# Two mixers read the raw stream; their norm's root is multiplied in behind the projections

## The chip, the cores and the metric

The kernel runs on 1 core of a Trainium2 chip. The metric is the time of one execution on the device, in microseconds (us); where several executions are timed, their median. Six things work side by side in the core, each through its own instruction list in order: TensorE (PE in the profile, with its weight loads as PEld), VectorE (DVE), ScalarE (ACT), GpSimd (POOL) and the queue on SyncE (SP) that issues the transfers. They meet only through semaphores: an instruction can be told to wait until another engine has counted one up.

## What is computed

Two transformer blocks run one after the other on one sequence of 256 tokens with 1024 features. Block 1 has a mixer and a feed-forward part. Block 2 has two layers; layer 0 mixes with a short convolution beside a forgetting attention, layer 1 with a conformer convolution module, and each is followed by a gated feed-forward part. Cut to what the change touches:

```python
def rms_norm_2(x, g):
    xf = x.astype(jnp.float32)
    y = xf * lax.rsqrt(jnp.mean(xf * xf, axis=-1, keepdims=True) + RMS_EPS)
    return (y * g.astype(jnp.float32)).astype(x.dtype)

def shortconv_fox_mixer(h, w_in, b_f, conv_w, w_out):
    proj = h @ w_in
    gate_b = proj[..., OFF_GB:OFF_GC]
    gate_c = proj[..., OFF_GC:OFF_XA]
    xa = proj[..., OFF_XA:OFF_Q]
    y_a = gate_b * causal_depthwise_conv(gate_c * xa, conv_w)
    ...
    log_f = jax.nn.log_sigmoid((proj[..., OFF_F:] + b_f).astype(jnp.float32))
    y_b = forgetting_attention(q, k, v, log_f).reshape(bsz, seq, D_FOX)
    return jnp.concatenate([y_a, y_b.astype(h.dtype)], axis=-1) @ w_out

def conformer_conv_module(h, w_pw1, b_pw1, w_dw, b_dw, ln_g, ln_b, w_pw2, b_pw2):
    a, g = jnp.split(h @ w_pw1 + b_pw1, 2, axis=-1)
    u = a * jax.nn.sigmoid(g)
    ...

def second_block(x, ...):
    h = x
    for layer in range(DEPTH_2):
        u = rms_norm_2(h, norm_mix_pre[layer])
        m = shortconv_fox_mixer(u, ...) if layer % 2 == 0 else conformer_conv_module(u, ...)
        h = h + rms_norm_2(m, norm_mix_post[layer])
        f = swiglu_ffn(rms_norm_2(h, norm_ffn_pre[layer]), w_ffn_in[layer], w_ffn_out[layer])
        h = h + rms_norm_2(f, norm_ffn_post[layer])
    return h
```

The norm divides every token by one number, its root. A matrix product is linear, so that factor may be applied to the product's result as well as to its input.

## The kernel before, in words

**Numbers in two halves.** Every large product is made of float32 numbers split into a high and a low part; three matrix multiplications (high·high, high·low, low·high) stand for one. The stream's halves lie in `H[0]` and `H[1]` (shown as H_h, H_l), 8 chunks of 128 features by 256 tokens. Weights arrive by DMA in units of 1 MB in the `raw` buffers; ACT copies a unit to `whi` (`split_hi`, L343), DVE subtracts to get `wlo` (`split_lo`, L350). There are two buffers of each, so the split of a unit waits until the unit two before it has been multiplied. `next_hi` and `next_lo` split the unit that follows the one named.

**Order of the work.** Each engine's list is written out by hand: `pe_program`, `act_program`, `dve_program` call one function per stage in the same order. The stages here are named after their weights: `down` (end of block 1), then layer 0's mixer `mix0` (`win2` units 6 to 11, the forget gate `wf2`, `win2` 0, then a run of eight attention jobs between which the remaining `win2` units are filled in), `wout2`, the feed-forward `ffn0` (`f0`, `g0`), layer 1's mixer `mix1` (`pw1`, the convolution by Fourier transform, a layer norm, `pw2`), and `ffn1` (`f1`, `g1`).

**From stage to stage.** A stage that ends in `wide_pe` (L1527) leaves its product in four PSUM banks, a token half `t` by a feature half `cb` each. DVE multiplies each by a row of gains (`mg_dve`, L1614, into `Mt`) and adds it to the stream `X` (`x_dve_add`, L1622, L1625); `X` has tokens on the partitions. PE turns `X` around (`turn_k`, L1652, a transpose of 128 by 128), ACT writes H_h with the norm's gain (`spread_act`, L1687), DVE writes H_l (`spread_dve`, L1692), and the next projection begins. `turnx_pe` does 12 of 16 transposes; the last four are a hook inside the first projection, which runs chunk by chunk as H arrives. While PE would wait, `spin_pe` (L432) makes it multiply for nothing.

**Two ways to norm.** Before `mix0` and `mix1` the norm is taken first: ACT squares `X` (L1542), makes the roots (`root_act`, L1551, L1554), and ACT and DVE write `X` times its root into `Mt` (`xs_act` L1564, `xs_dve` L1568); the transposes read `Mt`. Before `ffn0` and `ffn1` the transposes read `X` itself; ACT squares and takes the roots later, behind the next unit's split, PE makes a tile of them with one column per token (`rn_pe`, L1703, after the second projection unit), ACT copies it to `rn` (`rn_act`, L1711), and DVE multiplies `rn` in as it empties PSUM (L1837).

**Emptying PSUM in the mixers.** In `mix0` ACT empties most projections (`fox_act`, L1876 to L1889: gbt, gct, fq, fk), DVE only the values `fv` (L1910) and the product of the second gate (L1901). In `mix1` ACT takes the sigmoid of one half of a unit (L2210) and DVE multiplies the other half by it (L2243), both straight from PSUM.

Of the kernel before, what the change touches and what calls it, by code (L numbers as in the profile page):

```python
# [151 lines left out]
def build(nc, ins, out):  # L152
# [79 lines left out]
    place[0] = block2  # L232
    gbt, gct = sb("gbt", [128, 4, 256]), sb("gct", [128, 4, 256])
# [976 lines left out]
    def score_pe(pe, jobs, j, free):  # L1210
# [365 lines left out]
    def out_act(act, name, post, gen, scale):  # L1576
# [222 lines left out]
    def down_dve(dve):  # L1799
# [5 lines left out]
        out_dve(dve, "down", False, "mix0", True, lambda cb: mod_set(21 + 2 * cb), between)  # L1805
# [8 lines left out]
    def ffn_act(act, n, gen, name, rn_free=()):  # L1814
        for c in range(NF):
            next_hi(act, (n, c))
            if c == 0:
                for t in range(2):
                    xsq_act(act, name, gen, t, 0)
                    xsq_act(act, name, gen, t, 1)  # L1820
                    root_act(act, gen, t)
# [48 lines left out]
    def fox_act(act, i):  # L1870
        key = ("win2", i)
        next_hi(act, key)
        if i in (4, 5) or i >= 10:
            return
        act.wait_ge(*unit(*key))
        b, k = where[key], 2 * (i % 2)  # L1876
        if i < 2:
            act.activation(gbt[:, k:k + 2, :], v2(b[:]), ACT.Copy).then_inc(ev_act.hit("gb", i), 1)
        elif i < 4:
            act.activation(gct[:, k:k + 2, :], v2(b[:]), ACT.Copy).then_inc(ev_act.hit("gc", i), 1)  # L1880
        elif i < 8:
            act.mul(fq[:, k:k + 2, :], v2(b[:]), 0.125).then_inc(ev_act.hit("fq", i - 6), 1)
        else:
            if i == 8:
                act.wait_ge(*zeroed("fk"))
            for m in range(2):
                for e in range(2):
                    rw = slice(64 * e, 64 * e + 64)
# [709 lines left out]
```

## Time and profile before

| | |
|---|---|
| median of 3 runs | 1211.2 us (1208.37 to 1214.16) |
| the profiled execution's own time | 1211.38 us |
| its span in the trace | 1210.1 us |
| TensorE busy | 1151.7 us, 95% of the span |
| VectorE busy | 749.3 us, 62% |
| ScalarE busy | 600.7 us, 50% |
| mean granted TensorE clock | 0.974 of full speed |
| moved by DMA | 207.81 MB |

Busy shares are averages over stages with different limits. The profile also has the chain of waits: the chain of work that ended last, followed back from the last instruction, each piece with its start and length. An engine's piece stands there only when nothing else would have let the end come sooner.

### The profile page before, as it was taken

What the parts mean: (1) busy time and instruction counts of PE and PEld (TensorE: products, weight loads), DVE (VectorE), ACT (ScalarE), POOL (GpSimd) and SP (SyncE); (2) the same over time, 40 slices, a digit from 0 to 9 for tenths busy, and PEclk for the clock granted to TensorE, in tenths of its full rate; (3) what the DMA queues carried; (4) which work ended last, traced back from release to release, by engine and by line L of the source; (5) the groups of instructions that cost most, each with busy time, mean ns of one, the idle gap of its engine ahead of it and who ended that gap; (6) DMA issues with size and microseconds to landing.
All of it is one profiled execution on the core that took longest, in us unless ns stands there. A gap on an engine that the chain in (4) does not pass through costs nothing.

```text
span 1210.1 us, 19204 instructions
## 1 busy us (share of the span) xinstructions
PE 1151.7 (95%) x7762; PEld 1036.4 (86%) x7762; DVE 749.3 (62%) x1408; ACT 600.7 (50%) x1060; POOL 31.0 (3%) x32
## 2 busy tenths in 40 slices
PE   6899999899899999999998999999999999999998
PEld 3777989788779999888987799998878878999976
DVE  4655477788658788765466656665454446666644
ACT  2344466445456666445444564444464346544532
POOL 0411000000000000001000000000000000000000
PEclk9898999899899999999999999999999989999999
DMA  8757173245134555564542275554534304655450
GB/s 356 306 212 314 53 270 140 95 186 218 60 139 158 179 190 189 191 248 154 186 149 102 87 270 186 175 180 175 183 130 150 105 32 145 224 174 183 149 191 35
DMA packets 30508, 207.81 MB, mean 172 GB/s; under 512 B 3507, under 2 KB 4019, under 8 KB 6612
## 3 DMA queue, kind: packets, MB, share of 16 engines
q1 hardware_dynamic: 30420, 206.58, 47.1%
q8 instruction: 62, 1.02, 0.3%
q14 instruction: 26, 0.21, 0.1%
HBM read 205.52 MB, written 1.05 MB: 171 GB/s over the span
## 4 chain that ended last, share of the span: by engine, by line
PE 82%; DVE 9%; ACT 5%; issue 3%; DMA 1%; SPq 0%; ACTq 0%; DVEq 0%
PE ps L391 49%; PE ps L1527 18%; PE ps L409 2%; DVE wlo L350 2%; ACT whi L343 1%; PE ps L2144 1%; PE ps L2112 1%; DVE tm L558 1%; PE ps L1226 1%; ACT sq L1542 1%; PE ps L519 1%; PE ps L1304 1%; PE ps L755 1%; PE ps L1009 1%; DMA raw<-ada 1%
## 5 line engine op out<-in xcount | busy, mean ns | idle before, releaser
L350 DVE TENSOR_TENSOR wlo<-raw,whi 128x1024 fp32r<-128x1024 f32 x324 | 371.3, 1189 | 245.1 <-ACT whi L343 245.1
L391 PE MATMUL ps<-H_h,whi 128*128 128x256 f32 x1648 | 475.4, 288 | 4.1 <-DVE H_l L503 3.1
L391 PE MATMUL ps<-H_h,wlo 128*128 128x256 f32 x1648 | 469.3, 285 | 0.0
L391 PE MATMUL ps<-H_l,whi 128*128 128x256 f32 x1648 | 469.2, 285 | 0.0
L343 ACT ACTIVATE whi<-raw 128x1024 fp32r<-128x1024 f32 x324 | 315.0, 1022 | 154.9 <-PE ps L1527 111.8
L391 PEld LDWEIGHTS ps<-H_h,whi 128*128 128x128 f32 x1648 | 319.5, 194 | 9.2 <-issue 7.2
L391 PEld LDWEIGHTS ps<-H_l,whi 128*128 128x128 f32 x1648 | 319.6, 194 | 0.5 <-issue 0.2
L391 PEld LDWEIGHTS ps<-H_h,wlo 128*128 128x128 f32 x1648 | 319.2, 194 | 0.0
L1527 PE MATMUL ps<-whi,gl_h 128*128 128x512 f32 x264 | 105.3, 399 | 0.5 <-DVE wlo L350 0.5
L1527 PE MATMUL ps<-wlo,gl_h 128*128 128x512 f32 x264 | 104.3, 395 | 0.0
L1527 PE MATMUL ps<-whi,gl_l 128*128 128x512 f32 x264 | 104.3, 395 | 0.0
L1743 ACT ACTIVATE uw<-uw 128x256 f32<-128x256 f32 x66 | 27.5, 417 | 86.4 <-DVE uw L1837 86.4
L1527 PEld LDWEIGHTS ps<-whi,gl_h 128*128 128x128 f32 x264 | 49.6, 188 | 13.3 <-DVE wlo L350 1.4
L1527 PEld LDWEIGHTS ps<-wlo,gl_h 128*128 128x128 f32 x264 | 49.6, 188 | 12.1
L1527 PEld LDWEIGHTS ps<-whi,gl_l 128*128 128x128 f32 x264 | 49.6, 188 | 11.6
L1782 DVE SCALAR_TENSOR_TENSOR uw<-ps,par_sb,uw 128x255 f32<-128x255 f32 (+1 forms) x88 | 36.4, 477 | 25.2 <-ACT uw L1731 25.2
L1731 ACT ACTIVATE uw<-ps,par_sb 128x256 f32<-128x256 f32 x44 | 22.5, 562 | 46.4 <-PE ps L391 46.4
L558 DVE SCALAR_TENSOR_TENSOR tm<-raw,cs,tm 128x256 f32<-128x256 f32 x96 | 40.6, 480 | 0.0
L1837 DVE TENSOR_TENSOR uw<-ps,rn 128x512 f32<-128x512 f32 x44 | 30.2, 685 | 2.2 <-PE ps L391 1.9
L1753 ACT ACTIVATE gl_h<-tm 128x256 fp32r<-128x256 f32 x66 | 27.5, 417 | 2.7 <-DVE tm L1749 2.7
L1757 DVE TENSOR_TENSOR gl_l<-tm,gl_h 128x256 fp32r<-128x256 f32 x66 | 27.7, 420 | 0.8 <-ACT gl_h L1753 0.8
L1749 DVE TENSOR_TENSOR tm<-uw 128x256 f32<-128x256 f32 x66 | 27.7, 419 | 0.0
(416 smaller groups left out, 1421.7 us busy)
## 6 DMA issues: line engine op xcount, KB each, us to landing
raw<-f SPq DMA_DIRECT2D x44, 1024.0 KB, 4.9
raw<-win SPq DMA_DIRECT2D x33, 1024.0 KB, 6.3
raw<-ada SPq DMA_DIRECT2D x24, 1024.0 KB, 5.5
raw<-up SPq DMA_DIRECT2D x22, 1024.0 KB, 4.9
raw<-g SPq DMA_DIRECT2D x20, 1024.0 KB, 4.9
raw<-pw SPq DMA_DIRECT2D x12, 1024.0 KB, 4.9
raw<-down SPq DMA_DIRECT2D x10, 1024.0 KB, 5.7
raw<-ck SPq DMA_DIRECT2D x4, 1024.0 KB, 7.1
```

The costliest lines, as they stand in the source:

```text
L343: act.activation(whi[j % NS][:, a:b], raw_of(key)[:, a:b], ACT.Copy).then_inc(w_hi.hit(key, half), 1)
L350: dve.tensor_tensor(wlo[j % NS][:, a:b], raw_of(key)[:, a:b], whi[j % NS][:, a:b].bitcast(F32), ALU.subtract).then_inc(w_lo.hit(key, half), 1)
L391: ins_ = pe.matmul(bank[:, m * 256:(m + 1) * 256], wt[a][:, kt * w + col + m * 128:kt * w + col + m * 128 + 128], act[b][:, k0 + kt, :], s ...
L409: ins_ = pe.matmul(bank[:, t * width:(t + 1) * width], act[b][:, kt, t * 128:(t + 1) * 128], wt[a][:, kt * w + col:kt * w + col + width], ...
L558: dve.scalar_tensor_tensor(out=o, in0=w, scalar=cs[:, kt:kt + 1], in1=o, op0=ALU.mult, op1=ALU.add).then_inc(ada_sum.hit(u, kt), 1)
L1527: ins_ = pe.matmul(b[t][:], act[h][:, k0 + kt, t * 128:(t + 1) * 128], wt[a][:, kt * 512:(kt + 1) * 512], start=k0 + kt == 0 and i == 0 an ...
L1743: act.activation(w[:, g, :], w[:, g, :], ACT.Silu).then_inc(u_silu.hit(n, c), 1)
L1749: dve.tensor_tensor(x[:, 0:256], w[:, 0, :], w[:, 1, :], ALU.mult).then_inc(u_mul.hit(n, c), 1)
L1753: act.activation(gl[0][:, c, :], where["tm", n, c][:, 0:256], ACT.Copy).then_inc(g_hi.hit(n, c), 1)
L1757: dve.tensor_tensor(gl[1][:, c, :], where["tm", n, c][:, 0:256], gl[0][:, c, :].bitcast(F32), ALU.subtract).then_inc(g_lo.hit(n, c), 1)
L1782: dve.scalar_tensor_tensor(out=w[:, m, s:], in0=z[:, m, 0:256 - s], scalar=pc("w_conv", (2 * c + m) * 3 + 2 - s), in1=w[:, m, s:], op0=ALU ...
L1837: dve.tensor_tensor(uw[c % 3][:], v2(where[n, c][:]), bc2(rn[:]), ALU.mult).then_inc(u_rn.hit(n, c), 1)
```

## The change

In `mix0` and `mix1` the transposes now read `X`, as before `ffn0` and `ffn1`; the writes of `Mt` times a root, and the squares and roots ahead of the transposes, are gone. Squares and roots come behind the first `next_hi` of the mixer, `rn_pe` comes directly behind the mixer's first projection unit, and each projection is multiplied by `rn` as it leaves PSUM, all of it on DVE. The second gate's product takes the square of the roots, `rn2`. In `mix1` a new copy `zz` in SBUF is written in two halves, from which sigmoid and product read. `turnx_pe` is told to spin 0, 2 and 2 times instead of 7, 1, 1 and 14, 2, 1.

```diff
-                    else:
+                    elif scale:
                         xsq_act(act, name, gen, t, 0)
...
+    def xroots_act(act, name, gen):
+        for t in range(2):
+            xsq_act(act, name, gen, t, 0)
+            xsq_act(act, name, gen, t, 1)
+            root_act(act, gen, t)
...
-        out_dve(dve, "down", False, "mix0", True, lambda cb: mod_set(21 + 2 * cb), between)
+        out_dve(dve, "down", False, "mix0", False, lambda cb: mod_set(21 + 2 * cb), between)
...
     def fox_act(act, i):
-        key = ("win2", i)
-        next_hi(act, key)
-        if i in (4, 5) or i >= 10:
-            return
-        act.wait_ge(*unit(*key))
...
+        next_hi(act, ("win2", i))

     def fox_dve(dve, i):
         key = ("win2", i)
         next_lo(dve, key)
-        if i not in (4, 5) and i < 10:
-            return
         dve.wait_ge(*unit(*key))
         z, k = v2(where[key][:]), 2 * (i % 2)
+        if i == 6:
+            dve.wait_ge(*rn_set("mix0"))
+        if i < 2:
+            dve.tensor_tensor(gbt[:, k:k + 2, :], z, bc2(rn[:]), ALU.mult).then_inc(ev_dve.hit("gb", i), 1)
+        elif i < 4:
+            dve.wait_ge(*u_rn("square"))
+            dve.tensor_tensor(gct[:, k:k + 2, :], z, bc2(rn2[:]), ALU.mult).then_inc(ev_dve.hit("gc", i - 2), 1)
+        elif i < 6:
+            dve.wait_ge(*ev_dve("gc", i - 4))
             dve.tensor_tensor(gct[:, k:k + 2, :], gct[:, k:k + 2, :], z, ALU.mult).then_inc(f_gate.hit(i), 1)
+        elif i < 8:
+            dve.scalar_tensor_tensor(out=fq[:, k:k + 2, :], in0=z, scalar=0.125, in1=bc2(rn[:]), op0=ALU.mult,
+                                     op1=ALU.mult).then_inc(ev_dve.hit("fq", i - 6), 1)
+        elif i < 10:
...
+                ins_ = dve.tensor_tensor(dst, z[rw], bc2(rn[:])[rw], ALU.mult)
+            ins_.then_inc(ev_dve.hit("fk", i - 8), 1)
...
-                    ins_ = dve.tensor_copy(dst[:, t], src[:, t])
+                    ins_ = dve.tensor_scalar(dst[:, t], src[:, t], sv("mix0", 6 + t), None, ALU.mult)
...
     def mix0_pe(pe, hook):
         for i in range(6, 12):
             fox_pe(pe, i, hook if i == 6 else None)
+            if i == 6:
+                rn_pe(pe, "mix0")
...
         for i in range(6, 12):
             fox_act(act, i)
+            if i == 6:
+                xroots_act(act, "down", "mix0")
+                rn_act(act, "mix0")
...
-        dve.tensor_scalar(lt1[:], where["wf2", 0][0:8, 0:256], pc("b_forget")[0:8], None, ALU.add).then_inc(f_lf.hit(0), 1)
+        dve.tensor_tensor(lt1[:], where["wf2", 0][0:8, 0:256], rn[0:8, :], ALU.mult).then_inc(f_lf.hit("rn"), 1)
+        dve.tensor_tensor(rn2[:], rn[:], rn[:], ALU.mult).then_inc(u_rn.hit("square"), 1)
+        dve.wait_ge(*f_lf("rn"))
+        dve.tensor_scalar(lt1[:], lt1[:], pc("b_forget")[0:8], None, ALU.add).then_inc(f_lf.hit(0), 1)
...
     def mix1_pe(pe, hook):
         pe.wait_ge(*dft_in(1))
         for c in range(8):
...
+            if c == 0:
+                rn_pe(pe, "mix1")
...
+            if c == 0:
+                xroots_act(act, "g0", "mix1")
+                rn_act(act, "mix1", u_rn("f0", 21))
...
-            act.wait_ge(*unit("pw1", c))
+            act.wait_ge(*u_rn("pw1", c, 1))
...
+            for m in (1, 0):
+                mc = slice(m * 256, m * 256 + 256)
+                dve.tensor_tensor(zz[:, mc], where["pw1", c][:, mc], rn[:], ALU.mult).then_inc(u_rn.hit("pw1", c, m), 1)
+            dve.wait_ge(*u_rn("pw1", c, 0))
             dve.wait_ge(*ev_act("sig", c))
-            dve.scalar_tensor_tensor(out=x[:, 0:256], in0=where["pw1", c][:, 0:256], scalar=pc("b_pw1", 2 * c),
+            dve.scalar_tensor_tensor(out=x[:, 0:256], in0=zz[:, 0:256], scalar=pc("b_pw1", 2 * c),
...
-        turnx_pe(pe, "mix0", Mt, scaled("mix0"), n_lo, (7, 1, 1))
-        mix0_pe(pe, turn_late(pe, "mix0", Mt, scaled("mix0")))
+        turnx_pe(pe, "mix0", X, added("down"), n_lo, (0, 2, 2))
+        mix0_pe(pe, turn_late(pe, "mix0", X, added("down")))
...
-        turnx_pe(pe, "mix1", Mt, scaled("mix1"), n_lo, (14, 2, 1))
-        mix1_pe(pe, turn_late(pe, "mix1", Mt, scaled("mix1")))
+        turnx_pe(pe, "mix1", X, added("g0"), n_lo, (0, 2, 2))
+        mix1_pe(pe, turn_late(pe, "mix1", X, added("g0")))
...
-        out_act(act, "down", False, "mix0", True)
+        out_act(act, "down", False, "mix0", False)
...
-        out_act(act, "g0", True, "mix1", True)
+        out_act(act, "g0", True, "mix1", False)
...
-        out_dve(dve, "g0", True, "mix1", True, lambda cb: bc_in(3))
+        out_dve(dve, "g0", True, "mix1", False, lambda cb: bc_in(3))
```

How this moves the instructions of an engine is seen best in two places. The first is ACT's list from the last split of `down` to the third split in `mix0`; whi and raw are weights, sq and sst the squares and the roots of `X`. Before:

```order
L343 ACTIVATE whi_62<-raw_58 128x1024 x2
L1542 ACTIVATE sq_67,sst<-X 128x512
L1551 ACTIVATE sst<-sst 128x1
L1554 ACTIVATE sst<-sst 128x1
L1564 ACTIVATE Mt<-X,sst 128x512 x2
L1687 ACTIVATE H_h<-ps,par_sb 128x256 x8
L343 ACTIVATE whi_61<-raw_59 128x1024 x2
L1882 ACTIVATE fq<-ps 128x512
L343 ACTIVATE whi_62<-raw_60 128x1024 x2
```

(The second token half's squares, roots and `Mt` follow the first's in the same form.) Now:

```order
L344 ACTIVATE whi_62<-raw_58 128x1024 x2
L1688 ACTIVATE H_h<-ps,par_sb 128x256 x8
L344 ACTIVATE whi_61<-raw_59 128x1024 x2
L1543 ACTIVATE sq_67,sst<-X 128x512
L1546 ACTIVATE sst<-sst,epst 128x1
L1543 ACTIVATE sq_68,sst<-X 128x512
L1552 ACTIVATE sst<-sst 128x1
L1555 ACTIVATE sst<-sst 128x1
L1719 ACTIVATE rn<-ps 128x256
L344 ACTIVATE whi_62<-raw_60 128x1024 x2
```

Squares and roots (here too the second half follows the first) have moved from ahead of H_h to behind the split of the second unit, and fq is off the list. The list of `mix1` has the same shape.

The second place is DVE's list around the forget gate of `mix0`; lt is the gate's 8 rows, lf its turned copy. Before:

```order
L350 TENSOR_TENSOR wlo_63<-raw_60,whi_61 128x1024 x2
L2027 TENSOR_SCALAR lt_152<-ps,par_sb 8x256
L2029 TENSOR_SCALAR lt_153<-lt_153 8x256
L2031 SCALAR_TENSOR_TENSOR lt_152<-lt_152,lt_153 8x256
L350 TENSOR_TENSOR wlo_64<-raw_56,whi_62 128x1024 x2
L2035 COPY lf<-ps 128x16
```

Now:

```order
L351 TENSOR_TENSOR wlo_63<-raw_60,whi_61 128x1024 x2
L2033 TENSOR_TENSOR lt_153<-ps,rn 8x256
L2034 TENSOR_TENSOR rn_146<-rn 128x256
L2036 TENSOR_SCALAR lt_153<-lt_153,par_sb 8x256
L2038 TENSOR_SCALAR lt_154<-lt_154 8x256
L2040 SCALAR_TENSOR_TENSOR lt_153<-lt_153,lt_154 8x256
L351 TENSOR_TENSOR wlo_64<-raw_56,whi_62 128x1024 x2
L1885 TENSOR_TENSOR gbt<-ps,rn 128x512
L2044 COPY lf<-ps 128x16
```

Two multiplications stand ahead of the gate's first sum, and the emptying of `win2` 0 (gbt) ahead of the copy lf.

## Rows read from the trace of the kernel before

**Rows 1.** The page: busy time, share of the span and instructions of each engine.

```profile
PE 1151.7 (95%) x7762; PEld 1036.4 (86%) x7762; DVE 749.3 (62%) x1408; ACT 600.7 (50%) x1060; POOL 31.0 (3%) x32
```

**Rows 2.** Chain of waits, down to mix0: start us, length us, what.

```profile
564.29 0.71 PE ps L391 x6
```

**Rows 3.** Timeline of DVE, end of down: start us, length us, engine, line, operation, out<-in.

```profile
557.66 0.68 DVE L1614 TENSOR_TENSOR Mt<-ps,bc 128x512 f32<-128x512 f32 x1
```

**Rows 4.** Chain of waits, wout2 to ffn0, where X is turned itself.

```profile
691.24 0.70 DVE Mt L1614
691.99 0.77 PE ps L1652 x5
...
695.34 0.71 PE ps L391 x6
```

**Rows 5.** Timeline of PE, DVE and ACT, end of g0.

```profile
884.77 6.21 PE L432 MATMUL ps<-con_sb 128*128 128x256 f32 x28
885.24 0.20 ACT L1554 ACTIVATE sst<-sst 128x1 f32<-128x1 f32 x1
886.21 1.41 DVE L1622 SCALAR_TENSOR_TENSOR X<-Mt,sst,X 128x512 f32<-128x512 f32 x2
```

**Rows 6.** Chain of waits, g0 to mix1 and its first projection.

```profile
896.58 0.72 PE ps L391 x6
...
902.65 1.91 PE ps L2070 x4
```

**Rows 7.** Timeline of ACT in ffn0's first two units.

```profile
698.23 2.00 ACT L343 ACTIVATE whi<-raw 128x1024 fp32r<-128x1024 f32 x2
...
700.12 0.62 ACT L1542 ACTIVATE sq<-X 128x512 f32<-128x512 f32 x1
...
704.38 0.21 ACT L1554 ACTIVATE sst<-sst 128x1 f32<-128x1 f32 x1
...
707.65 0.39 ACT L1711 ACTIVATE rn<-ps 128x256 f32<-128x256 f32 x1 [1.16 <-PE ps L1703]
```

**Rows 8.** Chain of waits, ffn0: the tile of roots between two projections.

```profile
707.17 0.44 PE ps L1703 x4
```

**Rows 9.** Timeline of PE: two operations after idle time, which stands in brackets.

```profile
661.13 0.45 PE L1276 MATMUL ps<-con_sb,P 128*128 128x128 f32 x1 [3.00 <-DVE P L1260]
...
966.06 1.10 PE L2144 MATMUL ps<-Ya,dft 128*128 128x256 f32 x4 [2.24 <-DVE Ya L2132]
```

**Rows 10.** Windows: us, PE, PEld, DVE, ACT, POOL busy, PEclk granted, DMA share, GB/s.

```profile
660.50:661.00 0.50, 0.00 (x0) 0.00 (x0) 0.50 (x3) 0.00 (x0) 0.00 (x0) 0.50 1.22 197
...
667.00:667.50 0.50, 0.50 (x3) 0.37 (x3) 0.50 (x2) 0.00 (x0) 0.00 (x0) 0.92 0.00 0
```

**Rows 11.** The same, some microseconds after the third Fourier transform of mix1.

```profile
967.50:968.00 0.50, 0.50 (x3) 0.41 (x2) 0.00 (x0) 0.00 (x0) 0.00 (x0) 0.50 0.00 0
...
970.50:971.00 0.50, 0.50 (x3) 0.41 (x2) 0.17 (x1) 0.29 (x1) 0.00 (x0) 0.63 0.00 0
```

**Rows 12.** Chain of waits, the forget gate of mix0.

```profile
602.70 0.39 DVE lt L2027
...
608.10 0.10 DVE lf L2035
```

**Rows 13.** Timeline of PE: its wait for lf.

```profile
608.33 0.36 PE L1971 MATMUL ps<-lf,con_sb 128*128 128x8 f32 x2 [0.36 <-DVE lf L2035]
```

**Rows 14.** Timeline of DVE: prices of single operations on 128x256, and 8x256 in SBUF.

```profile
553.73 0.42 DVE L588 TENSOR_TENSOR bc<-bc,ps 128x256 f32<-128x256 f32 x1 [4.44 <-PE ps L574]
604.02 0.28 DVE L2029 TENSOR_SCALAR lt<-lt 8x256 f32<-8x256 f32 x1 [0.93 <-ACT lt L1995]
```

**Rows 15.** Timeline of ACT and DVE in mix0: emptying PSUM, a split, the attention's scores.

```profile
570.39 0.60 ACT L1882 ACTIVATE fq<-ps 128x512 f32<-128x512 f32 x1 [1.22 <-PE ps L391]
...
624.05 2.36 DVE L350 TENSOR_TENSOR wlo<-raw,whi 128x1024 fp32r<-128x1024 f32 x2 [1.16 <-ACT whi L343]
...
628.74 0.29 DVE L1237 CUSTOM_DVE_ANT_0 P<-ps,mh 128x128 f32<-128x128 f32 x1 [1.67 <-PE ps L1226]
```

More of the change, by code:

```diff
@@ L232, in build @@
     place[0] = block2
+    rn2 = sb("rn2", [128, 256])
     gbt, gct = sb("gbt", [128, 4, 256]), sb("gct", [128, 4, 256])
@@ L1220, in score_pe @@
         elif j.name[0] == "f" and j.name[1] % 2 == 0:
-            pe.wait_ge(*ev_act("fk", j.name[1] // 4))
+            pe.wait_ge(*ev_dve("fk", j.name[1] // 4))
         n = len(j.lhs)
@@ L1812, in ffn_pe, with ffn_act @@
                 rn_pe(pe, gen)
-    def ffn_act(act, n, gen, name, rn_free=()):
+    def ffn_act(act, n, gen, name, rn_free):
         for c in range(NF):
@@ L1817, in ffn_act @@
             if c == 0:
[L1818 to L1821, printed above, removed]
+                xroots_act(act, name, gen)
             if c == 1:
@@ L1870, in fox_act @@
     def fox_act(act, i):
-        key = ("win2", i)
-        next_hi(act, key)
-        if i in (4, 5) or i >= 10:
-            return
-        act.wait_ge(*unit(*key))
[L1876 to L1888, printed above, removed]
-                    ins_ = act.activation(fk[rw, 2 * (k + m) + e, :], b[rw, m * 256:(m + 1) * 256], ACT.Copy)
-            ins_.then_inc(ev_act.hit("fk", i - 8), 1)
+        next_hi(act, ("win2", i))
     def fox_dve(dve, i):
@@ L1952, in mix0_pe @@
             fox_pe(pe, i, hook if i == 6 else None)
-        b, old = G.take(f_lf(0))
+            if i == 6:
+                rn_pe(pe, "mix0")
+        b, old = G.take(f_lf("rn"))
         if old:
@@ L2173, in mix1_pe @@
         for c in range(8):
-            gemm_pe(pe, ("pw1", c), H, normed("mix1") if c == 0 else held, glu(c), by_k=c == 0, hook=hook if c == 0 else None)
+            gemm_pe(pe, ("pw1", c), H, normed("mix1") if c == 0 else held, u_rn("pw1", c, 0), by_k=c == 0, hook=hook if c == 0 else None)
+            if c == 0:
+                rn_pe(pe, "mix1")
             if c < 3:
@@ L2203, in mix1_act @@
                 conv_act(act, (c - 5) // 2)
+            if c == 0:
+                xroots_act(act, "g0", "mix1")
+                rn_act(act, "mix1", u_rn("f0", 21))
             buf, old = zt_ring.take(glu(c))
-            b = where["pw1", c]
-            act.wait_ge(*unit("pw1", c))
+            act.wait_ge(*u_rn("pw1", c, 1))
             if old:
@@ L2209, in mix1_act @@
             where["sig", c] = buf
-            act.activation(buf[:, 0:256], b[:, 256:512], ACT.Sigmoid, bias=pc("b_pw1", 2 * c + 1)).then_inc(
+            act.activation(buf[:, 0:256], where["zz", c][:, 256:512], ACT.Sigmoid, bias=pc("b_pw1", 2 * c + 1)).then_inc(
                 ev_act.hit("sig", c), 1)
@@ L2241, in mix1_dve @@
             x = temp(dve, ("tm", "glu", c), u_turn(c))
+            zz, old = rst_ring.take(glu(c))
+            where["zz", c] = zz
+            if c == 0:
+                dve.wait_ge(*rn_set("mix1"))
+            if old:
+                dve.wait_ge(*old)
+            dve.wait_ge(*unit("pw1", c))
+            for m in (1, 0):
+                mc = slice(m * 256, m * 256 + 256)
+                dve.tensor_tensor(zz[:, mc], where["pw1", c][:, mc], rn[:], ALU.mult).then_inc(u_rn.hit("pw1", c, m), 1)
+            dve.wait_ge(*u_rn("pw1", c, 0))
             dve.wait_ge(*ev_act("sig", c))
-            dve.scalar_tensor_tensor(out=x[:, 0:256], in0=where["pw1", c][:, 0:256], scalar=pc("b_pw1", 2 * c),
+            dve.scalar_tensor_tensor(out=x[:, 0:256], in0=zz[:, 0:256], scalar=pc("b_pw1", 2 * c),
                                      in1=where["sig", c][:, 0:256], op0=ALU.add, op1=ALU.mult).then_inc(glu.hit(c), 1)
@@ L2312, in act_program @@
         spread_act(act, "ffn0", lambda k: pc("ffn_pre", k))
-        ffn_act(act, "f0", "ffn0", "wout2")
-        out_act(act, "g0", True, "mix1", True)
+        ffn_act(act, "f0", "ffn0", "wout2", rn_free=ev_dve("gb", 1))
+        out_act(act, "g0", True, "mix1", False)
         mix1_act(act)
```

14 lines of the change are left out of this document (8 added, 6 removed).

## The prediction

> **What bounds the kernel now.** I read the busy shares first: TensorE works 95% of the span, so a change pays only where TensorE stands still on the chain of waits [rows 1]. I then read that chain around the two places that the change moves. At the end of `down`, DVE begins the last multiplication by the gains at 557.66 [rows 3], and the first product of `mix0` starts at 564.29 [rows 2]. The first product of `mix1` starts at 896.58 [rows 6], though `g0`'s products ended, and spins began, at 884.77 [rows 5]. In between run squares, roots and the write of `Mt`, one after the other. `wout2` to `ffn0` shows the form that the change copies: last multiplication at 691.24, then five transposes, spins, four transposes, spins, first product at 695.34 [rows 4]. That is 4.10 us, nearly all of it TensorE's own list once the bank is free.
>
> **The change part by part.**
>
> *The two passages.* With the form of [rows 4], `mix0` begins 4.10 us after 557.66, at 561.76: 564.29 - 561.76 = **2.5 us gained**. In `g0` the last multiplication then waits only for DVE itself. ACT's roots of the first half end at 885.44; with the squares of X gone, its squares of the last bank (near 0.8) follow at once and end near 886.3, while DVE is busy with two sums until 886.21 + 1.41 = 887.62 [rows 5]. So the last multiplication starts at 887.6, the first product at 891.7, and 896.58 - 891.7 = **4.9 us gained**. Together 7.4 us. The removed writes of `Mt` and the removed spins lie inside these gains and are not counted again.
>
> *The roots, later.* The squares and roots do not vanish. They stand behind H_h and one split on ACT, exactly as in `ffn0`: split at 698.23, first square at 700.12, last root done at 704.38 + 0.21 = 704.59 [rows 7]. Counted from the first product at 695.34 that is 9.25 us. But in `ffn0` PE asks for the roots after two projection units. In both mixers it asks after **one**, and one unit with its hook takes 902.65 - 896.58 = 6.07 us [rows 6]. TensorE therefore stands at `rn_pe` for 9.25 - 6.07 = 3.2 us, then makes the tile in 0.44 us [rows 8]: 3.6 to 3.7 us in each mixer, **7.4 us together**. What is queued behind the wait is the second unit of `win2`, and in `mix1` the first taps. So what the passages gain is handed back one projection later, almost to the tenth. Nothing hides this wait: TensorE's list holds no other work there, and ACT is busy from the split to the last root.
>
> *The clock.* A wait of that length behind dense work has a near match: TensorE idle for 3.00 us up to 661.13 [rows 9], and the granted clock is 0.50, that is 1.2 instead of 2.4 GHz, in a stretch that includes 660.5 and ends near 667.1 [rows 10]. A shorter wait, 2.24 us up to 966.06 [rows 9], is followed by full speed and then by 0.50 from about 967.5 to 970.7 [rows 11]. So a wait of 3.2 us costs between nothing and some 3 us more (half of the longer stretch). I take 1.3 us for each of the two, nearest to the shorter case: 3.2 us at half speed lose 1.6 if TensorE has work all through, and part of the stretch may fall into the wait. **2.6 us.** A third place is new: at the end of `g0` TensorE now idles from the last product at 884.8 until X's first quarter is added, near 886.9, and again for most of the time until the last bank is free at 888.3; spins stood there before [rows 5]. Bounds are zero and the same 1.6; I take **1.0 us**. The Trainium skill ("TensorE: Matmul & The Clock Gate", section "HAM oscillation") charges a wait like these half of the throttled time that follows, in full. By it the three places would cost 3 x 1.6 = 4.8 us instead of 3.6, and the sum would be 1.2 us higher; the trace shows the drop, but no row shows its whole price.
>
> *The forget gate.* Its chain starts with DVE at 602.70 and reaches the copy lf at 608.10 [rows 12], for which TensorE already waits 0.36 us [rows 13]. New in it: a multiplication by `rn` and one that makes `rn2`, each at most 0.42 by the nearest row; the gate's sum then reads SBUF, 0.28 [rows 14] instead of 0.39. That is 0.42 + 0.42 + 0.28 - 0.39 = 0.7, less near 0.2 since neighbours on DVE overlap: 0.5. Then gbt, 0.68 by [rows 3], stands in front of lf. **1.2 us**, all on the path.
>
> *Emptying on DVE.* fq costs near 0.68 [rows 3] instead of 0.60 on ACT [rows 15], fk two operations of at most that, fv four as before. DVE spends 2.36 us on a unit's split [rows 15] and has near 6 us a unit, so units 6 to 11 lose nothing; without that cover the price would be 0.7 to 1.4 us a unit. In `mix1` DVE takes on 2 x 0.42 a unit [rows 14], and TensorE asks for a unit's result only after the next one's products: nothing. The copy to `rn` starts near 0.5 us after the tile (707.17 to 707.65) and takes 0.39 [rows 7, 8], and the third unit's split (2.00 on ACT [rows 7], DVE half a unit behind) is done while TensorE is in the second: nothing. Among the attention jobs it is less clean. After a split, DVE used to weigh the previous job at once (split from 624.05, over at 626.4) and waited for TensorE only at the scores, 628.74 [rows 15]. Now it first waits for the projection and empties it, three times, and then weighs and takes the scores. TensorE needs the weighing a unit later, which covers most; where two jobs follow without a projection between, P comes late. Between 0 and 3 x 0.68 = 2.0 I take **0.5 us**, for only one such place.
>
> *No cost:* transfers are the same in number and size, and their queue waits for the splits, whose order stays. No activation table is loaded more often.
>
> Sum: -7.4 + 7.4 + 2.6 + 1.0 + 1.2 + 0.5 = **+5.3 us**. The profiled execution took 1211.38 us, 0.2 above the median of 1211.2. Made against it, this gives 1216.7; from the median 1216.5, and I forecast **1216.5 us**, 0.4% slower. A measurement of this kernel can tell about 0.5%, 6.1 us, from no change, so this may well read as no change.
>
> **The rivals.**
>
> *A. The roots are in time.* The passages' 7.4 us stand and the wait at `rn_pe` is not there. That is so if ACT's last root comes within 6.07 us of the first product. In `ffn0` it comes at 9.25 [rows 4, 7], and to be earlier ACT would have to square before its split or before H_h, which its list does not do. Then 1211.4 - 7.4 + 0.9 (two tiles) + 1.2 + 0.5 = 1206.6, or 1204.9 if DVE costs nothing: **faster**. Chance 0.06.
>
> *B. The waits come, the clock holds.* Nothing is lost beyond the waits, the gate and the jobs: 1211.4 + 1.2 + 0.5 = 1213.1. For it speaks that the passage of [rows 4] has waits too and its products follow at full speed; against it that waits of 3.00 and 2.24 us did bring the clock down [rows 9 to 11]. Chance 0.16.
>
> *C. DVE becomes the bound in `mix0`.* Its waits for projections push the weighing, the scores and ACT's splits in turn: all three emptyings land on the path (2.0), the wait for lf, now near 1.6, brings the clock down once more (up to 1.6), and both waits for the roots cost the longer stretch of [rows 10], 3 each: 1211.4 + 1.0 + 1.2 + 2.0 + 1.6 + 6.0 = 1223.2. DVE is at 62% of the span and ACT at 50% [rows 1], which speaks against a bound on DVE alone. Chance 0.10, with its neighbours above 1221.5. The Trainium skill ("TensorEngine Tiling (Array Packing)", section "PSUM Bottleneck") advises both ScalarE and VectorE for emptying PSUM, and this change puts `mix0`'s on one; by it C would be likelier than I hold it.
>
> *Forecast:* waits in both mixers, a slow stretch after them, gate and jobs as priced, 1213.5 to 1221.5. Chance 0.68.
>
> **How the numbers follow.** The range takes the forecast's span and half of B: **1212.5 to 1221.5**. It leaves out A, C and what lies just under B, near 2 in 10. Slower by over 0.5%, above 1217.3, is C (0.10) and a little under half of the forecast (0.30): 0.40. Faster by over 0.5%, below 1205.1, is the better part of A with a little for what I overlook: 0.05. The rest, 0.55, is no change that can be told.
>
> **What the profile after would show.** Right: 4.1 us from last multiplication to first product in both passages; TensorE's tile of roots waiting near 3.2 us for ACT in each mixer; PEclk at 0.50 for some microseconds after; TensorE's wait for lf near 1.6 us instead of 0.36. Wrong: no idle time ahead of the tile means A; full clock behind it means B; DVE instead of TensorE on the chain between the projections of `mix0` means C. If the passages do not shrink to 4.1 us, the first term was mis-sized.

## The result, and the profile after

The changed kernel takes 1222.9 us (median of 6 runs, 1222.1 to 1224.4) against 1210.8 us (6 runs, 1208.4 to 1214.2): ratio 1.0099, 95% interval 1.0081 to 1.0117, so 12.0 us or 1% slower. The forecast was 1216.5 us with a range up to 1221.5. It had the right sign and too small a size, and the measured time lies above the range. The profiled execution took 1222.05 us, its span 1220.8 us against 1210.1.

The page of the changed kernel, busy shares, answers to [rows 1]. VectorE has taken work from ScalarE, as the diff says:

```profile
PE 1153.4 (94%) x7734; PEld 1036.2 (85%) x7734; DVE 762.0 (62%) x1434; ACT 589.6 (48%) x1042; POOL 31.2 (3%) x32
```

Its chain of waits in `mix0` (start us, length us, what), against [rows 2, 12]:

```profile
561.91 0.71 PE ps L392 x6
...
570.94 0.21 ACT sst L1555
571.28 0.71 PE ps L1711 x4
571.99 18.74 PE ps L392 x144
590.73 11.53 PE ps L410 x96
...
605.80 0.32 DVE lt L2033
606.12 0.33 DVE rn L2034
...
611.73 0.60 DVE gbt L1885
612.56 0.37 PE ps L1974 x2
...
623.28 7.36 PE ps L392 x48
630.64 0.22 PE ps L1225 x2
...
657.06 0.22 PE ps L1225 x2
```

The same piece of the chain of the kernel before, from the gate's wait [rows 13] to the end of its first 48 products behind it, and the place that answers to 657.06:

```profile
614.55 5.95 PE ps L391 x48
620.50 0.22 PE ps L1224 x2
...
646.92 0.22 PE ps L1224 x2
```

The first product stands at 561.91 instead of 564.29, a gain of 2.4 us. From there the chain runs over ScalarE's squares and its last root to the tile of roots, L1711. The gate starts 3.1 us later than before (605.80 against 602.70), and TensorE has `lf` 4.2 us later (612.56 against 608.33). Then comes the surprise: from `lf` to the end of those 48 products it took 12.2 us before and takes 18.1 us now, with the same products. At 630.64 the kernel is 10.1 us late, which is most of the 12.

The chain in `mix1`, against [rows 6]:

```profile
901.67 0.72 PE ps L392 x6
...
911.05 1.19 PE ps L1711 x4
912.24 3.71 PE ps L2079 x4
915.95 7.72 PE ps L392 x48
923.67 1.91 PE ps L2079 x4
```

The first product is at 901.67, 5.1 us late instead of 10.1, so the passage out of `g0` did gain 5.0 us. At 923.67, where the kernel before was at 910.50, all of it is gone again and 3.1 us more: the four taps that took 1.91 us [rows 6] take 3.71. The line of the kernel before:

```profile
910.50 1.91 PE ps L2070 x4
```

TensorE's waits of the whole span (line, releaser, us in total, times, longest):

```profile
PE ps L1711 <- ACT sst L1555: 6.6, 2, 3.3
...
PE ps L1974 <- DVE lf L2044: 1.5, 1, 1.5
...
PE ps L1948 <- ACT lt L2007: 0.6, 1, 0.6
```

The last of them, for the gate's row of sums, stands behind the wait for `lf` and is as long in the kernel before:

```profile
PE ps L1947 <- ACT lt L2001: 0.6, 1, 0.6
```

And the windows of the changed kernel (us, busy us of PE, PEld, DVE, ACT and POOL, granted clock, DMA share, GB/s) behind the three waits, with the same windows of the kernel before under them:

```profile
572.00:576.00 4.00, 4.00 (x23) 4.00 (x23) 3.05 (x3) 2.27 (x3) 0.00 (x0) 0.60 0.00 0
612.00:627.00 15.00, 13.82 (x46) 9.34 (x47) 7.71 (x25) 4.30 (x12) 0.00 (x0) 0.54 0.19 71
...
910.00:920.00 10.00, 8.95 (x27) 6.21 (x28) 3.60 (x5) 5.81 (x11) 0.00 (x0) 0.50 0.45 165
```

```profile
572.00:576.00 4.00, 4.00 (x36) 4.00 (x35) 2.33 (x2) 0.88 (x1) 0.00 (x0) 1.00 0.20 39
612.00:627.00 15.00, 15.00 (x109) 13.07 (x108) 11.61 (x37) 7.86 (x18) 0.00 (x0) 1.00 0.22 77
...
910.00:920.00 10.00, 10.00 (x63) 7.60 (x61) 3.33 (x4) 5.76 (x10) 0.00 (x0) 1.00 0.38 135
```

The clock's figure is the reading that matters: 0.50 to 0.60, so at or near 1.2 GHz, where the kernel before has 1.00, 2.4 GHz. In 15 us behind the gate TensorE is busy for 13.8 us and the trace has 46 products, against 109 in the same window of the kernel before, which is some 4 us further on in its work.

**An account of clock and work.** In windows of 1 us I add up 2 x (1 - granted clock), which is the time at half speed, from the first product of `mix0` to 1200 us. Half of that time is lost where TensorE sets the pace. "Rest" is the time from that first product to the end of the span, less this half: what the kernel would need from there at full clock. Counting from the first product leaves out the stages ahead, in which nothing was changed and which differ by some us between the profiled executions. That half of the slow time is lost is an assumption here; the table of the gate, below, bears it out at one place, and kernel 12 shows a place where it does not hold.

| kernel | span | first product of `mix0` | half speed behind it | rest | rest against before |
|---|---|---|---|---|---|
| before | 1210.1 | 564.29 | 17.1 | 637.3 | |
| changed | 1220.8 | 561.91 | 37.6 | 640.1 | +2.8 |

The 13.1 us between the two from that point are 10.3 us of clock (half of 37.6 - 17.1) and 2.8 us of work and waits; 2.4 us had been gained ahead of it.

Each trace shows one execution, and the half speed is not the same in every execution of a kernel. Among 29 executions of the kernel before (those beside kernels 5 to 8), the mean granted clock is 0.980 in the six from 1208.3 to 1209.4 us and 0.972 in the two longest, 1216.9 and 1217.5 us. The profiled execution of the kernel before has 0.974, while the median of the 29 is 0.978; the changed kernel has 0.966 to 0.968 in all six. By 0.978 and 0.968 the change added some 25 us of half speed, and half of that, 12 us, is an estimate of its cost.

### The profile page after: what moved, and what is told of

It reads as the page before. It is cut to its first block, busy times and chain, and to the rows that moved or that the text cites. A ratio compares the mean times of both kernels' runs of the same rounds, so it can differ in the third digit from the quotient of the medians.

```text
span 1220.8 us, 19172 instructions
## 1 busy us (share of the span) xinstructions
PE 1153.4 (94%) x7734; PEld 1036.2 (85%) x7734; DVE 762.0 (62%) x1434; ACT 589.6 (48%) x1042; POOL 31.2 (3%) x32
## 4 chain that ended last, share of the span: by engine, by line
PE 82%; DVE 9%; ACT 6%; issue 3%; DMA 1%; SPq 0%; POOL 0%; ACTq 0%; DVEq 0%
PE ps L392 48%; PE ps L1528 18%; PE ps L410 2%; DVE wlo L351 2%; ACT whi L344 2%; PE ps L2153 1%; ACT sq L1543 1%; PE ps L2121 1%; PE ps L1227 1%; DVE tm L559 1%; PE ps L520 1%; PE ps L1653 1%; PE ps L1305 1%; PE ps L756 1%; PE ps L2079 1%
## 5 line engine op out<-in xcount | busy, mean ns | idle before, releaser
L392 PEld LDWEIGHTS ps<-H_h,whi 128*128 128x128 f32 x1648 | 321.8, 195 | 10.3 <-issue 8.6
```

The source lines that it names most:

```text
L392: ins_ = pe.matmul(bank[:, m * 256:(m + 1) * 256], wt[a][:, kt * w + col + m * 128:kt * w + col + m * 128 + 128], act[b][:, k0 + kt, :], s ...
```

## The experiments

The theory: new waits and operations cost about what was forecast; what is above it is half speed of TensorE's clock behind the new waits. The rivals: the extra time belongs to VectorE's new load (case C of the forecast), or to half speed that falls anywhere, whatever the waits are. All medians below stand beside runs of the kernel before on the same chip: 1210.7 us for the first four kernels, 1211.5 for the next four, 1211.6 for the last four.

**1 to 3. Filling the waits.** Idle products (seven took 3.2 us in kernel 3; constants times constants, result never read) stand ahead of the wait, so that it is spent busy; the wait itself stays. Kernel 1 fills the two waits for the roots, kernel 2 the two waits of the gate, kernel 3 all four.

```diff
# kernels 1 and 3, in rn_pe
+        for _ in range(7 if gen[0] == "m" else 0):
+            pe.matmul(b[:, 256:512], cc("ident"), con[:, 0:256], start=True, stop=True)
         pe.wait_ge(*rs(gen, 1))
# kernels 2 and 3
+        for _ in range(3):
+            pe.matmul(b[:, 256:512], cc("ident"), con[:, 0:256], start=True, stop=True)
         pe.wait_ge(*f_lf(3))
...
+        for _ in range(2 if h == 0 else 0):
+            pe.matmul(b[:, 256:512], cc("ident"), con[:, 0:256], start=True, stop=True)
         pe.wait_ge(*f_one("row"))
```

Kernel 1, waits for the roots: 

> The changed kernel with 7 spins (3.0 us of multiplying for nothing) ahead of TensorE's wait for the roots in mix0 and mix1. Theory 'clock': the two waits of 3.3 us stay, but the half-speed stretches behind them go, 1.8 us in mix0 and 4.4 us in mix1 by the changed kernel's trace, less what the tail of mix1 then loses again (its products fall back into slow stretches as before, up to 2.5): 1217 to 1219 us, against 1222.9. Rival 'VectorE': the loss is the emptying of PSUM on VectorE and its waits; spins change nothing: 1222 to 1224.

Kernel 2, waits of the gate: 

> The changed kernel with 3 spins ahead of TensorE's wait for lf and 2 ahead of its wait for the row of sums in the forget gate of mix0; the waits for the roots untouched. Theory 'clock': full speed from 612 to 627 of the changed kernel's trace, 4.5 to 6 us less, so 1217 to 1218.5 us. Rival 'VectorE': nothing, 1222 to 1224; if the spins are longer than the waits, up to 1 us more.

Kernel 3, all: 

> Both sets of spins. Theory 'clock': what is left above the kernel before is waits and the gate's longer chain alone, 1211.5 to 1214.5 us. Rival 'VectorE': 1221 to 1224.

Measured: kernel 1, 1220.4 us (ratio to before 1.0087, 1.0066 to 1.0109); kernel 2, 1221.3 us (1.0092, 1.0067 to 1.0116); kernel 3, 1212.7 us (1.0018, 1.0004 to 1.0033). With all four waits filled 10.2 of the 12 us are gone, though the kernel does more work, not less. The windows of kernel 3:

```profile
572.00:576.00 4.00, 3.81 (x29) 3.36 (x28) 1.56 (x2) 3.08 (x7) 0.00 (x0) 1.00 0.01 2
612.00:627.00 15.00, 15.00 (x92) 11.45 (x92) 9.48 (x33) 4.79 (x13) 0.00 (x0) 1.00 0.27 80
...
910.00:920.00 10.00, 10.00 (x72) 8.62 (x72) 5.53 (x7) 5.79 (x10) 0.00 (x0) 1.00 0.40 118
```

Kernels 1 and 2 are misses in size: each gave 1.6 to 2.4 us where 4 to 6 were expected. Their windows say why. In kernel 1 the filled places are at 1.00, but the end of `g0`, at full speed in the changed kernel, is now in part at half:

```profile
572.00:576.00 4.00, 4.00 (x36) 4.00 (x35) 3.05 (x3) 2.28 (x3) 0.00 (x0) 1.00 0.00 0
612.00:627.00 15.00, 14.38 (x52) 10.53 (x51) 7.68 (x23) 4.31 (x12) 0.00 (x0) 0.54 0.23 80
...
892.00:904.00 12.00, 9.22 (x40) 7.42 (x39) 8.30 (x13) 5.36 (x15) 0.95 (x1) 0.72 0.26 88
```

Kernel 2 reads 0.86 in that last window too, while its gate is at 1.00 for all of 612 to 627 us. So a wait that is left open is a place at which the clock may fall, in one arrangement and not in another, and with one place repaired the fall can turn up at another. The idle time at the end of `g0`, where the change took spins away, is such a place. What decides whether the clock falls there is not shown.

**4. No wait for the roots.** The tile takes the roots of an earlier norm, which are long there, so its wait is gone, and the normed values of both mixers are scaled by other roots. All other work stays.

```diff
+        src = {"mix0": "F", "mix1": "ffn0"}.get(gen, gen)
+        if src == gen:
+            pe.wait_ge(*rs(gen, 1))
...
-            ins_ = pe.matmul(b[:, t * 128:(t + 1) * 128], sv(gen, 6 + t).to_broadcast([128, 128]), cc("ident"), start=True,
+            ins_ = pe.matmul(b[:, t * 128:(t + 1) * 128], sv(src, 6 + t).to_broadcast([128, 128]), cc("ident"), start=True,
```

> The changed kernel in which TensorE makes the tile of roots of mix0 and mix1 from the roots of an earlier norm (those of block 1's feed-forward and of ffn0), which are there already, and so does not wait; everything else, ScalarE's squares and roots too, is done as in the changed kernel. The projections of both mixers are thus scaled by another norm's roots. Theory 'waits hand back the gain': two waits of 3.3 us and the slow stretches behind them (1.8 and 4.4) go, and the stretch at lf (5.9) may stay: 1210 to 1214 us. Rival: the third unit's weights are split behind the roots on ScalarE and TensorE then waits for those instead; 1218 or more.

Measured: 1213.2 us (1.0017, 1.0004 to 1.0031), within the expectation and far from its rival's 1218. The rest of the account falls by 6.0 us against the changed kernel (634.1 against 640.1), near the two waits of 3.3 us. And behind the gate there are still 13.7 us at half speed (table below), so that stretch needs no wait for the roots ahead of it.

**5 and 6. Each half of the change alone.** Kernel 5 has the new `mix0` and the old `mix1`, kernel 6 the reverse.

```diff
# kernel 5, against the changed kernel
-        turnx_pe(pe, "mix1", X, added("g0"), n_lo, (0, 2, 2))
+        turnx_pe(pe, "mix1", Mt, scaled("mix1"), n_lo, (14, 2, 1))
...
-        out_act(act, "g0", True, "mix1", False)
+        out_act(act, "g0", True, "mix1", True)
```

Kernel 5: 

> The change in the first mixer alone: the second mixer takes the normed stream again, with the code of before. The theory (the time is the changed steps plus half-speed stretches behind each new wait): the changed kernel spent in the second mixer -5.0 us of passage, +3.7 us of wait and tile, +4.4 us of half-speed stretch, and -2.5 us because the stretches at its attention jobs fell elsewhere, +0.6 us together; all else, some 10 us, is in the first mixer. So 1220 to 1223 us. Rival (the half-speed stretches fall anywhere, whatever the waits are): between 1214 and 1224 us. The clock's row should be at half speed behind the first roots' wait and behind the forget gate as in the changed kernel, and nowhere between 890 and 930 us.

Kernel 6: 

> The change in the second mixer alone: the first mixer and its forget gate are those of before. The theory: -5.0 us of passage, +3.7 us of wait and tile, +4.4 us of half-speed stretch behind the roots' wait, -2.5 to 0 us at the attention jobs behind it: 1211 to 1214 us, and the clock's row of the first mixer at full speed throughout as before. Rival (a wait is worth only its own length, the clock is no part of it): 1209.5 us.

Measured: kernel 5, 1220.8 us (1.0074, 1.0049 to 1.0099); kernel 6, 1216.4 us (1.0035, 1.0017 to 1.0053). Kernel 5 is as expected: most of the loss is in the first mixer. Kernel 6 is 2.4 us above its expectation. Its gate is at full speed as before; its window at the end of `g0` is not, which I had not put into the number. It is 3.4 us at half speed, at most 1.7 of the 2.4 us. The trace is of the slowest of its twelve executions, 1219.35 us:

```profile
612.00:627.00 15.00, 14.13 (x91) 11.30 (x92) 9.49 (x35) 6.70 (x20) 0.00 (x0) 1.00 0.33 103
...
892.00:904.00 12.00, 10.79 (x69) 9.81 (x69) 7.34 (x13) 7.49 (x18) 0.00 (x0) 0.86 0.15 64
910.00:920.00 10.00, 10.00 (x51) 8.86 (x51) 2.83 (x4) 2.25 (x5) 0.00 (x0) 0.66 0.32 107
```

**7. The tile one unit later.** As in the feed-forward blocks, TensorE makes the second unit's products before it asks for the roots; VectorE empties the first two units together, and in `mix1` the gated product of the first unit comes behind the second unit too.

```diff
-            if i == 6:
+            if i == 7:
                 rn_pe(pe, "mix0")
...
+        if i == 7:
+            fox_empty(dve, 6)
+        if i != 6:
+            fox_empty(dve, i)
...
-            if c == 0:
+            if c == 1:
                 rn_pe(pe, "mix1")
```

> The changed kernel with the roots' tile made one unit later in both mixers, as the kernel's feed-forward blocks do: the second unit's products stand ahead of the wait for the roots, and the first unit is emptied after the second. The theory: both waits of 3.3 us go, and the stretches at half speed behind them (1.8 and 4.4 us); the wait of the forget gate and its stretch of 5.9 us stay: 1209 to 1212.5 us. Rival (VectorE, with its emptyings pushed together, becomes the bound of the fq and fk units): a new wait of TensorE for a PSUM bank or for wlo in the units 2 to 7, and over 1214 us.

Measured: 1213.3 us (1.0009, 0.9993 to 1.0026), 0.8 above the expectation. The chain of waits shows the tile between two runs of products, with nothing ahead of it, and no bound by VectorE:

```profile
565.14 9.35 PE ps L392 x78
574.49 0.45 PE ps L1711 x4
574.93 11.51 PE ps L392 x96
```

The rival (VectorE as the bound, over 1214 us) is out: TensorE has no new wait in the units of `mix0`. What is left against the kernel before is the gate: 0.61 in the window 612 to 627 us, and 0.72 at the end of `g0`.

**8. A shorter gate chain.** To kernel 7: `gbt` is emptied behind the copy of `lf`, and `rn2` is made while ScalarE works.

```diff
-        dve.tensor_tensor(rn2[:], rn[:], rn[:], ALU.mult).then_inc(u_rn.hit("square"), 1)
         dve.wait_ge(*f_lf("rn"))
...
+        dve.tensor_tensor(rn2[:], rn[:], rn[:], ALU.mult).then_inc(u_rn.hit("square"), 1)
         dve.wait_ge(*f_one("exp"))
...
-        fox_dve(dve, 0)
+        next_lo(dve, ("win2", 0))
         dve.wait_ge(*f_turn())
         dve.tensor_copy(lf[:], where["lf"][:, 0:16].rearrange("p (t h) -> p t h", t=2)).then_inc(f_lf.hit(3), 1)
+        fox_empty(dve, 0)
```

> The kernel with the late tile, and two VectorE operations taken out of the forget gate's chain: unit win2 0 is emptied behind the copy of lf and not ahead of it (0.60 us), and rn2 is made while ScalarE does the exponential (0.33 us). The theory: the gate's chain is then as short as in the kernel before, TensorE's wait at lf falls to under 0.6 us and the clock is full behind it: 7 us under the kernel with the late tile alone, or 1203 to 1206 us. Rival (what fell was the clock behind the small products of the gate, whatever the wait ahead of them): some 0.9 us under the kernel with the late tile, with half speed from 610 us on as in it.

Measured: 1209.5 us (0.9983, 0.9966 to 0.9999). That is 3.5 us above the expectation. The wait at `lf` fell to 0.7 us, not under 0.6, and the half speed behind it to 6.8 us from 13.7, so the truth lies between the two cases. In the window 612 to 627 us:

```profile
612.00:627.00 15.00, 15.00 (x87) 12.82 (x86) 8.50 (x31) 6.36 (x17) 0.00 (x0) 0.77 0.19 71
```

**9 and 10. The wait at the gate by itself, on the kernel before.** Nothing of the change is in these two. VectorE makes six, or two, more small copies ahead of `lf`.

```diff
+    lfx = sb("lfx", [128, 8, 2, 8])
...
         dve.wait_ge(*f_turn())
+        for q in range(6):
+            dve.tensor_copy(lfx[:, q], where["lf"][:, 0:16].rearrange("p (t h) -> p t h", t=2))
```

Six copies: 

> The kernel before, with six more copies of 16 columns (0.17 us each, into a tile that nobody reads) on VectorE ahead of the copy of lf, so that TensorE's wait at the forget gate grows from 0.36 to some 1.5 us, the changed kernel's, and nothing else changes. The theory (the length of this wait decides on the clock behind it): half speed for 10 to 14 us from 610 us on, and +1.1 us of wait and +5 to +7 us of clock, 1216 to 1220 us. Rival (the half speed there comes of the change's other operations, or of where in time the gate falls): full clock behind the gate, and 1212 us.

Two copies: 

> The same with two copies: a wait of about 0.7 us. The theory, by the kernel with the shortened gate chain (0.7 us of wait, 6.8 us of half speed): +0.4 us of wait and about half the stretch, +3 us: 1213.5 to 1216 us. Rival (a threshold above 0.7 us): full clock, 1211.5 us.

Measured: six copies 1216.7 us (1.0046, 1.0029 to 1.0062), two copies 1212.7 us (1.0006, 0.9992 to 1.0021). The copies overlap and took 0.08 us each (chain, first row below), so the wait grew only to 0.8 and 0.5 us. With six, the chain, TensorE's wait and the window:

```profile
610.01 0.49 DVE lfx L2037 x6
```

```profile
PE ps L1972 <- DVE lf L2038: 0.8, 1, 0.8
```

```profile
612.00:627.00 15.00, 14.38 (x65) 11.23 (x63) 8.20 (x26) 4.31 (x12) 0.00 (x0) 0.66 0.31 123
```

Half a microsecond more on VectorE's chain cost 5.1 us. This is the disputed cost by itself: no change of the norm, no wait for roots, no load on VectorE to speak of. What it does not take apart is the second wait, 0.6 us for the gate's row, which stands behind `lf` in this kernel as in every one that leaves the gate open; kernels 2, 3, 11 and 12 fill both. Whether a longer wait for `lf` would do it without the second is open. With two copies the window has 1.00 in the profiled execution and no loss can be told from the medians: 0.8 us under the expectation, on the side of the rival, though at 0.5 us and not at 0.7.

All kernels at this place, from their chains and windows, one profiled execution each:

| kernel | wait at `lf`, us | half speed behind it, us | first product behind `lf` to end of the 48 products, us |
|---|---|---|---|
| before; kernel 6 | 0.4 | 0 | 12.2; 12.2 |
| 10, two copies | 0.5 | 0 | 12.2 |
| 8, short chain | 0.7 | 6.8 | 15.2 |
| 9, six copies | 0.8 | 10.2 | 16.7 |
| 5, `mix0` alone | 1.5 | 10.2 | 16.8 |
| changed; 1; 4; 7 | 1.5 | 13.6 to 13.7 | 18.1; 18.1; 18.0; 18.2 |
| 2; 3; 11; 12, waits filled | none | 0 | 12.6, with 0.4 for the idle products ahead of the row |

Where the waits are open, the last column exceeds 12.2 by 0.43 to 0.46 times the column before it. Here half speed is paid for in nearly half its length.

**11 and 12. Versions that beat both.** Kernel 11 is kernel 8 with one idle product ahead of `lf` and two ahead of the gate's row. Kernel 12 adds six ahead of the last attention job of `mix0`, where both kernels wait 3.0 us [rows 9] and the clock falls [rows 10].

```diff
+            for _ in range(6 if jobs is FOX and m == len(jobs) - 1 else 0):
+                pe.matmul(b[:, 0:256], cc("ident"), con[:, 0:256], start=True, stop=True)
             pe.wait_ge(*snorm(j.name, 2))
```

Kernel 11: 

> The kernel with the late tile and the short gate chain, with one idle product of 256 columns ahead of TensorE's wait for lf and two ahead of its wait for the gate's row. The theory: the 6.8 us at half speed behind the gate go, for 0.3 us of products that are too long for the wait: 3 us under the kernel without them, 1206 to 1207.5 us, and faster than both kernels. Rival (the half speed only moves to the next wait, the 3.0 us one of the last attention job or the end of g0): 1209 to 1210 us with as many us of half speed as without.

Kernel 12: 

> The same, and six idle products (2.3 us) ahead of TensorE's wait of 3.0 us for the last attention job of the first mixer, behind which the kernels before and after both have 6.8 us at half speed. The theory: that stretch goes too where TensorE sets the pace there; TensorE is idle for part of it, so 1 to 3 us under the kernel without these products: 1204 to 1206.5 us. Rival (TensorE at half speed is hidden there, since the chain runs over VectorE and ScalarE): no difference.

Measured, both inside what was expected: kernel 11, 1206.8 us (0.9956, 0.9940 to 0.9972); kernel 12, 1205.1 us (0.9951, 0.9932 to 0.9969). Both are faster than the kernel before, by 5 to 6 us by their ratios, and than the changed one by 16 or more, measured in another series of runs. Their runs overlap (1204.4 to 1207.4 and 1202.2 to 1207.4), so they can't be told apart. The window that kernel 12 aims at, first in kernel 11 and then in kernel 12:

```profile
660.00:670.00 10.00, 6.90 (x22) 5.54 (x23) 8.05 (x21) 2.20 (x6) 0.00 (x0) 0.66 0.27 105
```

```profile
660.00:670.00 10.00, 7.97 (x38) 6.12 (x36) 8.38 (x21) 2.33 (x6) 0.00 (x0) 1.00 0.31 105
```

The clock is repaired. The products of `wout2`, behind the last attention job, start, again in kernel 11 and then in kernel 12, at

```profile
673.81 17.08 PE ps L1528 x72
```

```profile
674.36 17.08 PE ps L1530 x72
```

which is 110.0 us after the first product of `mix0` (563.77 and 564.31) in both, and from that first product to the end of the span it is 641.8 us in both. TensorE does not set the pace there, so half speed cost nothing in these traces. That is the rival of kernel 12, though its median lies where the theory had it; the runs overlap too much for the medians to decide, and the profiled execution of kernel 12 is the slowest of its six.

**The account for all kernels**, made as above (us):

| kernel | half speed | rest against before | forecast's terms for it |
|---|---|---|---|
| changed | 37.6 | +2.8 | -4.9 + 7.4 + 1.2 + 0.5 = +4.2 |
| 1, 2, 3: waits filled | 30.7, 30.7, 13.6 | +3.1, +3.8, +4.9 | +4.2, and what the fillers overrun |
| 4, borrowed roots | 27.3 | -3.2 | -4.9 + 0.9 + 1.2 + 0.5 = -2.3 |
| 5, `mix0` alone | 27.3 | +4.3 | 3.7 + 1.2 + 0.5 = +5.4 |
| 6, `mix1` alone | 27.3 | -1.1 | -4.9 + 3.7 = -1.2 |
| 7, late tile | 30.7 | -3.7 | -2.3 |
| 8, short gate | 20.5 | -3.4 | -2.3 - 0.6 - 0.3 = -3.2 |
| 9, 10: copies | 23.9, 17.0 | +0.7, +0.1 | +0.5, +0.2 by their chains |
| 11, 12 | 17.1, 10.2 | -4.0, -0.6 | near -3; removed half speed that had cost nothing in 12 |

The terms without the clock come out within 1.5 us everywhere but in kernel 12, where half the removed slow time is subtracted though it cost nothing; the time at half speed ranges over 27 us. The gain of `mix0`'s passage, 2.5 us, lies ahead of the count and is in none of these terms.

## Why the prediction was wrong, point by point

- **The passages, -7.4.** Right. From the last multiplication (557.84) to the first product in `mix0` it takes 4.07 us, forecast 4.10. The gains are 2.4 and 5.0 us, forecast 2.5 and 4.9.
- **The wait for the roots, +7.4.** Right: 3.3 us twice, forecast 3.2, and the tile of 0.44 on top. (The forecast's own terms, 3.18 and 0.44 twice, add up to 7.2, not 7.4.) Kernels 4 and 7, with the wait gone in two different ways, lose 6.0 and 6.5 us of rest.
- **The gate, +1.2.** Right in length: TensorE's delay grew from 3.10 us at 605.80 to 4.23 at 612.56, so +1.13, and the wait became 1.5 us, forecast near 1.6.
- **Emptying among the attention jobs, +0.5.** It cost nothing: the delay is 10.1 us at 630.64 and still 10.1 at 657.06, where 646.92 stood before. TensorE's products stand on the chain up to there in both kernels, so a later P held nothing up.
- **The clock behind the waits for the roots, +2.6.** Mis-sized. In `mix0` the tile to the first products of the values (`fv`, L410) takes 571.28 to 590.73, 19.45 us, and 17.98 in kernel 1 with the wait filled: 1.5 us, forecast 1.3. In `mix1` it is 12.62 us to the second taps, against 8.56 in kernel 1: 4.1 us, forecast 1.3. I had taken the shorter of two stretches and halved it; in `mix1` the stretch was 10.2 us, longer than either of the two that I had read, and nearly nine of them fell behind the wait, on work of TensorE. The lines of kernel 1:

```profile
571.26 0.71 PE ps L1713 x4
571.97 17.27 PE ps L392 x144
589.24 11.54 PE ps L410 x96
...
912.12 0.71 PE ps L1713 x4
...
920.68 1.91 PE ps L2081 x4
```

- **The clock at the end of `g0`, +1.0.** The idle time came as forecast, 2.2 us until the first sum, but there is no half speed behind it in the changed kernel's profile, and 3.4 to 6.8 us of it in kernels 1, 2, 6, 7, 11 and 12. As a chance it was right, as a cost of this kernel not.
- **The clock behind the gate, nothing.** This is the step that failed. I priced the gate as a matter of length alone ("1.2 us, all on the path"), although the same text put TensorE's wait there at 1.6 us and held a wait of 2.24 us to be enough for a fall. It stood only in case C, at 1.6 us and 1 in 10. It cost 5.9 us (18.1 against 12.2), more than any other term of the clock, and kernel 9 gets 4.5 us of it by half a microsecond of wait.
- What was given back: the half speed in the window 965 to 1000 us became less (0.95 against 0.85), and the delay fell from 13.2 us to 10.6 (1003.88 against 993.24). The forecast had nothing of that. No run takes it apart: over all fourteen kernels this window reads between 0.85 and 0.95.

The clock's terms then are 1.5 + 5.9 + 4.1 less some 2.5 given back: 9.0 us, where 3.6 was forecast. Between the profiled executions (1222.05 - 1211.38 = 10.7 us, forecast 5.3) 5.4 us were missing; the clock is 5.4 of them, the emptying that cost nothing takes 0.5 off, and some 0.5 stays unexplained. The medians are 1.3 us further apart, which is within the spread of the runs of the kernel before.

Case C came near in time, 1223.2, by another sum: 6.0 for the clock behind the roots (measured 5.6), 1.6 for the clock behind the gate (5.9), 2.0 for the emptyings (nothing), and a bound on VectorE that kernel 7 does not show. Case B, the clock at full speed, is near to kernel 3: 1213.1 forecast, 1212.7 measured. That they agree so closely is in part luck, since kernel 3 also runs idle products and has 3.5 us less half speed in its account than the kernel before.

The Trainium skill ("TensorE: Matmul & The Clock Gate", section "HAM oscillation"), by which half of the throttled time is lost in full, was cited for 1.2 us more than my sum. The trace agrees with it behind the gate (0.43 to 0.46 of the stretch) and in `mix1` (4.1 of 10.2 us), and does not at the last attention job, where kernel 12 removes 6.8 us of half speed and gains nothing in its trace.

## What to carry to other kernels

Price a wait of TensorE twice: its own length, and, where TensorE's list is the chain, half of the slow stretch that may follow, and do the second for every wait that the change lengthens, above all for a small one ahead of dense work. The cure is to ask late (kernel 7), to shorten what is ahead of the wait (kernel 8), or to fill it with idle products (kernel 3); fill all such waits together, since with one filled the clock can fall at another that is open. Where a change only moves a chain out of one gap, as here the squares and roots, look where it comes to lie: with the second unit's products ahead of the wait, the same change would be worth some 6 us at full clock. That is an estimate, 2.4 us ahead of `mix0`'s first product and 3.7 behind it by the account; kernel 11, with the gate's chain shortened and its waits filled on top, is 4.9 us faster than the kernel before.

## What the runs showed of the hardware

A wait grown from 0.4 to 0.8 us (kernel 9) brought 10.2 us at half speed, and one of 0.5 us (kernel 10) brought none in the profiled execution; waits of 1.5 us brought 10.2 to 13.7 us. So a short wait did not cost little: most of the price was there at 0.8 us. Behind the gate TensorE is busy for most of the time (13.8 of 15 us in the changed kernel) and the clock still reads 0.54 there; the rows do not tell which of the small products or gaps in that stretch kept it low, and no run here takes them apart.
